# A diffusion backbone's first modulation: three chunks streamed with the vectors stationary, one summed by VectorE, h in two parts, and pair 1's sums between its panels

## Chip, cores, metric

The kernel runs on one core of a Trainium2 chip. The metric is the device time of one execution in microseconds.

## The reference, cut to what matters

Two layers act on 512 latent and 256 context tokens of width 1024, in float32. Each layer has nine modulation vectors per token kind; they come from a vector `c` (latent) or `c_ctx` (context) and a 1024 x 9216 matrix. The first half FFN needs vectors 0 (shift), 1 (scale) and, at its end, 2 (gate) of layer 0.

```
mx = (silu(c) @ ada_w[i] + ada_b[i]).reshape(B, 1, N_MOD, D_MODEL)
mc = (silu(c_ctx) @ ada_w[i] + ada_b[i]).reshape(N_MOD, D_MODEL)
h  = rms_norm(x, norm_g[i, 0]) * (1.0 + mx[:, :, 1]) + mx[:, :, 0]
u  = h @ w_gu
x  = x + 0.5 * mx[:, :, 2] * ((silu(u[..., :D_FF]) * u[..., D_FF:]) @ w_down)
```

After four such half FFNs, one attention and pooling mixer and one recurrent mixer (RG-LRU, whose decay rates come from a softplus of a small vector `lam`) comes a final norm.

## The kernel before

Features lie on the 128 partitions and tokens along the free axis. `resid` holds x and ctx as 8 tiles of 128 x 768. Each engine has its own program; they meet only through semaphores. Panels of weights (1024 x 128) are loaded by the SP queue into one of two raw buffers, ScalarE makes a rounded high part (`high`, L738), GpSimd the low part (`low`, L643), and TensorE multiplies in three passes: high by high, high by low, low by high. The activations h have such parts too, `h_hi` and `h_lo`. A panel of 768 tokens is 8 k-tiles x 3 passes x 2 halves of 384 tokens, so 48 matmuls of 384 columns.

**The prologue.** SP loads x and ctx, then the small vectors, then the first 2048 columns of the modulation matrix (`ada_first`) in four chunks of 2 MB (L479): chunks 0 and 1 are the shift, 2 and 3 the scale, 512 columns each. TensorE transposes x (L1729), VectorE copies it to `resid` (L1292), ScalarE squares (L784), VectorE adds up the squares (L1085). Then TensorE takes chunk 0 with the *weights* stationary and the two vectors `cvec` moving, two columns at a time (L1739, 32 products of 128x128 by 128x2), then the column sums of squares (L1674) and the spreading of 1/rms over the partitions (L1684), which lead through VectorE's `statistics` (L1141), and then chunk 1. VectorE meanwhile multiplies and adds up chunks 2 and 3 (`first_ada`, L1256, through `sum_tiles`, L1026), and TensorE adds these sums over partitions with a vector of ones (L1749). A float32 matmul stands in the trace as two records.

When all 16 tiles are in, VectorE adds the bias (L1267), makes `mod_a` (L1016), and then for each token half (384) and each k: scale (`scale_rows`, L1165), high part on ScalarE (L811), low part on VectorE (L1176). In the second half each of these is two instructions, since latent tokens end at column 512. Behind these rows VectorE computes the decay rates for the recurrent layer (L1304 to L1318), after ScalarE's Exp (L891).

**The first panels.** TensorE begins the first half FFN with `first_panels` (L1594): panel A on half 0, panel B on half 0, panel A on half 1, panel B on half 1, each k-tile waiting for its rows of h. The gate panel goes to `pair_a`, the up panel to `pair_b`; the two are pair 0. Then `gate_up` (L1629) runs pairs 1 to 10. Pair 0 and every later pair end with `use_ada` (L1619): 4 products (8 records) with ones that turn the sums of the next two modulation tiles into columns. VectorE makes such sums in `sum_ada` (L1041) at the head of each pair, and takes the result at the pair's end (`take_ada`, L1046).

**The SP queue's order.** Of each pair SP issues the load of panel A, then `load_ada` (L489), which waits until the previous sums are made, and then the load of panel B. So B's load stands behind VectorE's sums. After the loop of pairs come the down panels `dn00`, then the second half of the FFN, `gu01` and `dn01`.

## Time and profile before

| | us |
|---|---|
| median of 3 runs | 2909.53 |
| range of the runs | 2909.39 to 2911.92 |
| the profiled execution, own time | 2915.29 |
| its span, first to last instruction | 2913.5 |
| TensorE busy in the span | 2767.8 (95%) |
| VectorE busy | 1485.7 (51%) |
| ScalarE busy | 772.6 (27%) |
| GpSimd busy | 896.8 (31%) |
| mean granted TensorE clock, 1 = 2.4 GHz | 0.967 |

PE is TensorE's matmuls, PEld its weight loads, DVE VectorE, ACT ScalarE, POOL GpSimd, SPq the queue on which SP issues DMAs. In a timeline each row is a group of like instructions: its start, the time from its first start to its last end, engine, line, operation, and in brackets how long the engine was idle before it and what ended that. A busy TensorE is not TensorE at its full clock: the granted clock has to be read beside it.

### The profile page before, as it was taken

Reading aid. Unit: us, or ns where it says so; the run is one execution under the profiler, and the core shown is the slowest. Engines: PE = TensorE matmul, PEld = TensorE weight load, DVE = VectorE, ACT = ScalarE, POOL = GpSimd, SP = SyncE. Lnnn points to the kernel's source line nnn. Section 1 sums busy time; section 2 is a strip of 40 time slices with the busy share of each in tenths; the row PEclk is TensorE's granted clock in tenths of the full one; section 3 lists DMA queues with packets and bytes.
Section 4 is the critical chain, followed back from the end, with each engine's and each line's share of the span. In section 5 each row is a group of like instructions: output and inputs, shape, how many; then the busy total and the mean of one; then the engine's idle time right before and its main releaser. Section 6 shows DMA issues by size and latency. Waiting matters only on the chain.

```text
span 2913.5 us, 40217 instructions
## 1 busy us (share of the span) xinstructions
PE 2767.8 (95%) x15161; PEld 2597.9 (89%) x15161; DVE 1485.7 (51%) x2553; ACT 772.6 (27%) x1039; POOL 896.8 (31%) x360
## 2 busy tenths in 40 slices
PE   6799999999999989999999999999998887899998
PEld 6799999998965989999999899999997775778887
DVE  5655555655535366655665523522238887432233
ACT  1322111112145232211111322111125665332222
POOL 0133222332222223322332223222223444244442
PEclk6899999999999999999999999999998997999999
DMA  5244334432210234434443122312211112223332
GB/s 197 58 127 129 111 101 126 127 100 69 68 61 19 65 88 115 123 100 116 115 123 107 44 65 80 107 58 61 75 52 40 55 54 57 70 86 107 88 101 79
DMA packets 413083, 256.77 MB, mean 88 GB/s; under 512 B 6653, under 2 KB 405846, under 8 KB 413014
## 3 DMA queue, kind: packets, MB, share of 16 engines
q1 hardware_dynamic: 413014, 255.87, 30.4%
q8 instruction: 40, 0.66, 0.1%
q14 instruction: 29, 0.24, 0.0%
HBM read 252.70 MB, written 4.25 MB: 88 GB/s over the span
## 4 chain that ended last, share of the span: by engine, by line
PE 65%; issue 19%; DVE 6%; POOL 5%; ACT 4%; DMA 0%; SPq 0%; POOLq 0%; DVEq 0%; ACTq 0%
PE pair_b L1575 28%; PE pair_a L1575 28%; POOL w_lo L647 5%; PE pair_c L1625 2%; PE pair_c L1854 1%; PE pair_a L1815 1%; DVE decay L1535 1%; PE pair_b L1829 1%; DVE decay L1533 1%; PE pair_a L1565 1%; DVE gate_i L1529 1%; DVE h_lo L1176 1%; DVE root L1527 1%; ACT decay L975 1%; ACT root L977 1%
## 5 line engine op out<-in xcount | busy, mean ns | idle before, releaser
L647 POOL TENSOR_TENSOR w_lo<-raw,w_hi 128x1024 fp32r<-128x1024 f32 (+3 forms) x302 | 829.5, 2748 | 1796.7 <-ACT w_hi L750 1796.7
L750 ACT ACTIVATE w_hi<-raw 128x1024 fp32r<-128x1024 f32 (+3 forms) x302 | 337.2, 1117 | 1281.1 <-PE pair_b L1575 443.7
L1067 DVE TENSOR_TENSOR work_g<-work_s,pair_b 128x768 f32<-128x768 f32 (+1 forms) x88 | 78.1, 888 | 702.2 <-PE pair_b L1575 539.7
L1037 DVE SCALAR_TENSOR_TENSOR ada_sums<-ada_raw,cvec,ada_sums 128x256 f32<-128x256 f32 x896 | 395.7, 515 | 0.0
L1575 PE MATMUL pair_a<-h_hi,w_hi 128*128 128x384 f32 x1312 | 338.3, 338 | 9.6 <-POOL w_lo L647 9.6
L1575 PE MATMUL pair_a<-h_lo,w_hi 128*128 128x384 f32 x1312 | 333.6, 335 | 0.0
L1575 PE MATMUL pair_a<-h_hi,w_lo 128*128 128x384 f32 x1312 | 333.6, 335 | 0.0
L1575 PE MATMUL pair_b<-h_hi,w_hi 128*128 128x384 f32 x1168 | 297.7, 335 | 5.9 <-POOL w_lo L647 5.9
L1575 PE MATMUL pair_b<-h_hi,w_lo 128*128 128x384 f32 x1168 | 297.6, 335 | 0.0
L1575 PE MATMUL pair_b<-h_lo,w_hi 128*128 128x384 f32 x1168 | 297.5, 335 | 0.0
L1575 PEld LDWEIGHTS pair_a<-h_hi,w_hi 128*128 128x128 f32 x1312 | 234.5, 189 | 13.5 <-issue 9.6
L1575 PEld LDWEIGHTS pair_a<-h_lo,w_hi 128*128 128x128 f32 x1312 | 237.5, 188 | 0.0
L1575 PEld LDWEIGHTS pair_a<-h_hi,w_lo 128*128 128x128 f32 x1312 | 237.5, 188 | 0.0
L1575 PEld LDWEIGHTS pair_b<-h_hi,w_hi 128*128 128x128 f32 x1168 | 211.7, 189 | 6.5 <-POOL w_lo L647 6.5
L1575 PEld LDWEIGHTS pair_b<-h_lo,w_hi 128*128 128x128 f32 x1168 | 211.9, 189 | 0.0
L1575 PEld LDWEIGHTS pair_b<-h_hi,w_lo 128*128 128x128 f32 x1168 | 211.9, 189 | 0.0
L1098 DVE SCALAR_TENSOR_TENSOR resid<-pair_b,mod_g,resid 128x512 f32<-128x512 f32 (+3 forms) x74 | 42.3, 603 | 314.4 <-PE pair_b L1575 245.2
L1565 PE MATMUL pair_b<-h_hi,w_hi 128*128 128x512 f32 (+3 forms) x352 | 140.0, 398 | 33.3 <-DVE gelu L1514 33.1
L1073 DVE TENSOR_TENSOR g_lo<-work_g,g_hi 128x768 f32 (+1 forms) x88 | 147.3, 1673 | 10.8
L1566 PE MATMUL pair_b<-h_lo,w_hi 128*128 128x512 f32 (+3 forms) x352 | 137.5, 391 | 0.0
L1565 PE MATMUL pair_a<-h_hi,w_hi 128*128 128x512 f32 (+2 forms) x280 | 115.7, 413 | 22.8 <-DVE h_lo L1176 19.2
L1567 PE MATMUL pair_b<-h_hi,w_lo 128*128 128x512 f32 (+3 forms) x352 | 136.8, 389 | 0.0
(272 smaller groups left out, 4548.5 us busy)
## 6 DMA issues: line engine op xcount, KB each, us to landing
raw<-in_ffn_w_gu_dram SPq DMA_DIRECT2D x176, 512.0 KB, 3.9
ada_raw<-in_ada_w_dram SPq DMA_DIRECT2D x64, 1024.0 KB, 5.2
raw<-in_ffn_w_down_dram SPq DMA_DIRECT2D x64, 704.0 KB, 5.5
raw<-in_rg_w_in_dram SPq DMA_DIRECT2D x20, 512.0 KB, 3.8
ada_first<-in_ada_w_dram SPq DMA_DIRECT2D x4, 2048.0 KB, 18.0
raw<-in_ab_w_in_dram SPq DMA_DIRECT2D x16, 512.0 KB, 3.8
raw<-in_rg_w_out_dram SPq DMA_DIRECT2D x8, 640.0 KB, 4.6
raw<-in_ab_w_out_dram SPq DMA_DIRECT2D x8, 512.0 KB, 4.1
```

The costliest lines, as they stand in the source:

```text
L647: nc.gpsimd.tensor_tensor(wl[:, par, 0:kt * P], raw[:, par, 0:kt * P], wh[:, par, 0:kt * P].bitcast(F32), ALU.subtract).then_inc(split_rea ...
L750: nc.scalar.activation(wh[:, par, 0:kt * P], raw[:, par, 0:kt * P], ACT.Copy).then_inc(hi_done, 1)
L975: nc.scalar.activation(decay[d][:, :], gate_r[d][:, :], ACT.Exp, bias=rg_scale[:, m:m + 1], scale=rg_scale[:, m:m + 1])
L1037: step = nc.vector.scalar_tensor_tensor(out=sums[v], in0=tiles(k), scalar=c_k, in1=sums[v], op0=ALU.mult, op1=ALU.add)
L1067: nc.vector.tensor_tensor(gbuf[:, 0, 0:W], sbuf[:, 0, 0:W], up, ALU.mult)\
L1073: nc.vector.tensor_tensor(gl[:, ds(i, 1), 0:W].rearrange("p o n -> p (o n)"), gbuf[:, 0, 0:W], gh[:, ds(i, 1), 0:W].rearrange("p o n -> p ...
L1098: return nc.vector.scalar_tensor_tensor(out=resid[:, k, a:b], in0=src, scalar=mod_g[:, SITE[name], k, v:v + 1], in1=resid[:, k, a:b], op0= ...
L1565: nc.tensor.matmul(dst, w1, hi, start=start, stop=False)
L1566: nc.tensor.matmul(dst, w1, lo, start=False, stop=False)
L1567: return nc.tensor.matmul(dst, w2, hi, start=False, stop=stop)
L1575: last = nc.tensor.matmul(tokens(ps, a, a + HALF), w, of[:, k, a:a + HALF], start=begins, stop=ends)
L1625: last = nc.tensor.matmul(pC[:, 2 * t + v:2 * t + v + 1], ada_sum[:, v, t * P:(t + 1) * P], ones[:, 0:1], start=True, stop=True)
```

## The change

- **TensorE.** Chunks 2, 3 and 1 are now taken with the two vectors stationary (a 128x2 operand) and 512 columns of weights moving, 8 products each, into a 2 x 512 row block of PSUM (`ada_rows`). ScalarE copies each block to SBUF (`copy_ada0`) and TensorE turns it into four 128x2 columns (`turn_ada`).
- **VectorE** sums chunk 0 only, in two parts of four k with `statistics` between.
- **Order.** SP loads chunks 2, 0, 3 ahead of the first two weight panels and chunk 1 behind them. TensorE: chunk 2, both sums of squares, chunk 3, its turning and both spreadings, chunk 0's sums, chunk 1, the last turnings.
- **h in two parts.** k 0 to 3 of both token halves are made once the first four shift and scale tiles are there, k 4 to 7 of both halves after the rest; `row_number` gives the new counts.
- **GpSimd** waits for VectorE's chunk 0 sums before the first low part.
- **Pair 1** is written out: `use_ada(8)`, formerly after pair 0, stands between its panels A and B.
- **Decay rates** with their Exp move from ahead of the first FFN to behind `dn00`.

```diff
@@ -217,7 +217,8 @@
         pro = alias(h_at, g_at)
         xin = pro("x_rows", [P, T // P, D])
         rowbuf = pro("vector_rows", [P, 3, P])
-        ada0_sum = pro("ada_first_sums", [P, 2, 2, ADA0_W])
+        ada0_sum = pro("ada_first_sums", [P, 2, ADA0_W])
+        ada0_row = at("ada_first_rows", [P, 3, ADA0_W], F32, h_at + size([P, KD, T]) + size([P, KD // 2, T]))
         ada0 = alias(g_at, g_end)("ada_first", [P, KD, 2 * ADA0 * P])
...
@@ -305,6 +306,11 @@
         ada_landed = sem("ada_landed")
         ada_summed = sem("ada_summed")
         ada0_summed = sem("ada0_summed")
+        ada0_mm = sem("ada0_mm")
+        ada0_copied = sem("ada0_copied")
+        ada0_turned = sem("ada0_turned")
+        mods_first = sem("mods_first")
+        coef_first = sem("coef_first")
...
@@ -403,6 +409,12 @@
         def norm_tiles_before(i):
             return sum(width(name) // P for name in NORMS[:i])
 
+        def row_number(i, half, k):
+
+            if i > 0:
+                return KD * (2 * i + half) + k
+            return k // 4 * KD + half * 4 + k % 4
+
...
@@ -476,9 +488,14 @@
             rows(lam.rearrange("o d (k p) -> (o d k) p", p=P), R_LAM, 2 * KR)
             assert landed[0] == ROW_DMAS, landed[0]
             w0 = ada_w[0].rearrange("(k p) n -> p k n", p=P)
-            for i in range(4):
+
+            def load_ada0(i):
                 chunk = slice(i * ADA0_W, (i + 1) * ADA0_W)
                 sp.dma_start(ada0[:, :, chunk], w0[:, :, chunk]).then_inc(ada0_landed[i], 16)
+
+            load_ada0(2)
+            load_ada0(0)
+            load_ada0(3)
...
@@ -518,6 +535,7 @@
                     if p0 == 0:
                         load(0, 0, KD, gu[:, :, 0:P])
                         load(1, 1, KD, gu[:, :, DFF:DFF + P])
+                        load_ada0(1)
                         load_ada(ADA0, ADA0, 0)
                         pad_rpb()
                     with_ada(ada_first.get(f"gu{f}{h}"), int(p0 == 0), KC, gate_up)
...
@@ -660,6 +678,7 @@
                 pairs(first[f"gu{f}1"], 0, KC, KD)
                 pairs(first[f"dn{f}1"], 0, KD // 2, KC)
 
+            pool.wait_ge(ada0_summed, 2 * KD)
             ffn(0)
             low(P_AB, 0, KD)
             low(P_AB + 1, 1, KD)
...
@@ -805,7 +824,7 @@
             def high_rows(name, half, k):
 
                 i = NORM_AT[name]
-                act.wait_ge(scaled_done, 2 * KD * i + KD * half + k + 1)
+                act.wait_ge(scaled_done, row_number(i, half, k) + 1)
                 t = shift_tile(i) + k
                 for v, a, b in spans(name, half):
                     last = nc.scalar.activation(hh[:, k, a:b], normed[k % 4][:, a:b], ACT.Identity, bias=mods[:, t, v:v + 1])
...
@@ -868,6 +887,10 @@
                 for h in range(2):
                     gate_up(f, h)
                     outputs(f"dn{f}{h}", first[f"dn{f}{h}"])
+                    if f == 0 and h == 0:
+
+                        act.wait_ge(lam_exp, 1)
+                        nc.scalar.activation(lam_s[:, 1, :], lam_s[:, 0, :], ACT.Exp, scale=-1.0).then_inc(lam_exp, 1)
 
 
             act.wait_ge(cols_done, 1)
@@ -878,17 +901,28 @@
...
@@ -878,17 +901,28 @@
             chain(nc.scalar.activation(sd[:, 7:8], ones[:, 0:1], ACT.Sqrt))
             for k in range(KD):
                 square("in", k)
+
+            def copy_ada0(n, ps, c0):
+
+                act.wait_ge(ada0_mm, n + 1)
+                nc.scalar.activation(ada0_row[0:2, n, :], ps[0:2, c0:c0 + ADA0_W], ACT.Copy).then_inc(ada0_copied, 1)
+
+            copy_ada0(0, pR, 512)
             for half in range(2):
                 root_half("in", half)
             high(0)
             high(1)
+            copy_ada0(1, pB, 0)
+            act.wait_ge(coef_first, 2)
+            for half in range(2):
+                for k in range(4):
+                    high_rows("in", half, k)
+                    if half == 1 and k == 1:
+                        copy_ada0(2, pB, 512)
             act.wait_ge(coef_done, 2)
             for half in range(2):
-                for k in range(KD):
+                for k in range(4, KD):
                     high_rows("in", half, k)
-
-            act.wait_ge(lam_exp, 1)
-            nc.scalar.activation(lam_s[:, 1, :], lam_s[:, 0, :], ACT.Exp, scale=-1.0).then_inc(lam_exp, 1)
             ffn(0)
 
 
...
@@ -1023,9 +1057,9 @@
                 nc.vector.tensor_scalar(mod_g[:, site, :, :], mods[:, t:t + KD, :], 1.0 if site % 3 == 1 else 0.5, None,
                                         ALU.mult).then_inc(coef_done, 1)
 
-            def sum_tiles(tiles, sums, signal, before):
-
-                for k in range(KD):
+            def sum_tiles(tiles, sums, signal, before, ks=range(KD)):
+
+                for k in ks:
                     for v in range(2):
                         n = 2 * k + v
                         c_k = cvec[:, k, v:v + 1]
...
@@ -1160,7 +1194,7 @@
                     dve.wait_ge(rbc_done, norm_tiles_before(i) + half_of(name, half)[1] // P)
                 if k >= 4:
 
-                    dve.wait_ge(h_ready, 2 * KD * i + KD * half + k - 3)
+                    dve.wait_ge(h_ready, row_number(i, half, k - 4) + 1)
                 for v, a, b in spans(name, half):
                     last = nc.vector.scalar_tensor_tensor(out=normed[k % 4][:, a:b], in0=resid[:, k, a:b],
                                                           scalar=mod_a[:, i, k, v:v + 1], in1=halved(pR, name, a, b),
...
@@ -1253,26 +1287,73 @@
                 nc.vector.memset(pT[:, :, PADW - 8:PADW], 0.0).then_inc(proj_done, 1)
                 nc.vector.memset(pT[:, :, PAD_X + SEQ:PAD_C], 0.0).then_inc(proj_done, 1)
 
-            def first_ada():
+            def take_ada0(g):
+
+                tiles = slice(4 * g, 4 * g + 4)
+                src = pC[:, 0:4 * ADA0].rearrange("p (s t v) -> p s t v", s=2, v=2)
+                for v in range(2):
+                    last = nc.vector.tensor_tensor(mods[:, 0:2 * ADA0, v].rearrange("p (s t) -> p s t", s=2)[:, :, tiles],
+                                                   src[:, :, tiles, v],
+                                                   cols[:, 0:2 * ADA0].rearrange("p (s t) -> p s t", s=2)[:, :, tiles], ALU.add)
+                last.then_inc(mods_first if g == 0 else mods_done, 1)
+                dve.wait_ge(mods_first if g == 0 else mods_done, 1)
+                done = coef_first if g == 0 else coef_done
+                for v in range(2):
+                    nc.vector.scalar_tensor_tensor(out=mod_a[:, 0, tiles, v], in0=mods[:, KD:2 * KD, v][:, tiles], scalar=1.0,
+                                                   in1=cols[:, R_NORM:R_NORM + KD][:, tiles], op0=ALU.add, op1=ALU.mult)\
+                        .then_inc(done, 1)
+                dve.wait_ge(done, 2)
+
+            def first_rows():
 
                 dve.wait_ge(silu_done, 1)
+                dve.wait_ge(ada0_landed[0], 16)
+
+                def sums(ks):
+                    sum_tiles(lambda k: ada0[:, k, 0:ADA0_W], [ada0_sum[:, v, :] for v in range(2)], ada0_summed, 0, ks)
+
+                sums(range(4))
+                dve.wait_ge(ss_done, 2)
                 for half in range(2):
-                    dve.wait_ge(ada0_landed[2 + half], 16)
-                    c0 = (2 + half) * ADA0_W
-                    sum_tiles(lambda k: ada0[:, k, c0:c0 + ADA0_W], [ada0_sum[:, half, v, :] for v in range(2)],
-                              ada0_summed, 2 * KD * half)
-                dve.wait_ge(ada_used, 1)
-                src = pC[:, 0:4 * ADA0].rearrange("p (t v) -> p v t", v=2)
-                for v in range(2):
-                    last = nc.vector.tensor_tensor(mods[:, 0:2 * ADA0, v], src[:, v, :], cols[:, 0:2 * ADA0], ALU.add)
-                last.then_inc(mods_done, 1)
-
-                dve.wait_ge(mods_done, 1)
+                    statistics("in", half)
+                sums(range(4, KD))
+                for g in range(2):
+                    if g == 0:
+                        dve.wait_ge(ada0_turned, 1)
+                    else:
+                        dve.wait_ge(ada_used, 1)
+                    take_ada0(g)
+                    for half in range(2):
+                        for k in range(4 * g, 4 * g + 4):
+                            scale_rows("in", half, k)
+                            if k % 4:
+                                low_rows("in", half, k - 1)
+                        low_rows("in", half, 4 * g + 3)
+
+            def decay_rates():
+
+                dve.wait_ge(lam_exp, 2)
...
```

## Rows read from the trace of the kernel before

**Rows 1.** The profile's page: busy time of each engine, share of the span, instructions.
```profile
PE 2767.8 (95%) x15161; PEld 2597.9 (89%) x15161; DVE 1485.7 (51%) x2553; ACT 772.6 (27%) x1039; POOL 896.8 (31%) x360
```
**Rows 2.** Timelines of the prologue, and two 512-column float32 products of a later stage.
```profile
25.95 13.65 PE L1739 MATMUL pair_c<-cvec,ada_first 128*128 128x2 f32 x64
...
70.36 3.57 PE L1749 MATMUL pair_c<-ones,ada_first_sums 128*128 128x1 f32 x16 [6.20 <-DVE ada_first_sums L1037]
...
825.58 1.02 PE L1795 MATMUL pair_c<-p_t,pool_weights 128*128 128x512 f32 x2
826.44 0.59 PE L1796 MATMUL pair_c<-p_t,pool_weights 128*128 128x256 f32 x2
```
**Rows 3.** Windows: length, busy PE, PEld, DVE, ACT, POOL, clock, DMA share, GB/s.
```profile
50.00:60.00 10.00, 10.00 (x49) 10.00 (x48) 10.00 (x14) 0.00 (x0) 1.08 (x1) 0.50 0.18 52
...
82.00:84.00 2.00, 2.00 (x9) 1.47 (x9) 1.85 (x5) 0.61 (x1) 0.00 (x0) 0.77 0.00 0
...
103.00:105.00 2.00, 0.00 (x0) 0.00 (x0) 2.00 (x7) 0.00 (x0) 0.00 (x0) 0.60 0.00 0
...
860.00:880.00 20.00, 20.00 (x108) 12.09 (x108) 10.99 (x38) 10.76 (x27) 1.30 (x3) 1.00 0.03 7
```
**Rows 4.** The tile `ada_first`: time from issue to landing of its four loads.
```profile
DMA to landing us min/median/max: 12.5/18.0/19.9
```
**Rows 5.** Timeline of the prologue: VectorE's steps and the low parts of GpSimd.
```profile
28.05 2.02 DVE L1085 TENSOR_TENSOR sum_sq<-sum_sq,work_s 128x768 f32<-128x768 f32 x2
...
40.92 0.16 DVE L1147 TENSOR_SCALAR mean_sq<-pair_c 128x3 f32<-128x3 f32 x1 [10.86 <-PE pair_c L1674]
...
41.57 0.68 DVE L1153 TENSOR_SCALAR sum_sq<-ident,rstd 128x128 f32<-128x128 f32 x3
...
45.90 2.98 DVE L1033 TENSOR_SCALAR ada_first_sums<-ada_first,cvec 128x512 f32<-128x512 f32 x2
46.09 4.98 POOL L647 TENSOR_TENSOR w_lo<-raw,w_hi 128x1024 fp32r<-128x1024 f32 x2 [44.61 <-ACT w_hi L750]
...
60.16 0.87 DVE L1033 TENSOR_SCALAR ada_first_sums<-ada_first,cvec 128x512 f32<-128x512 f32 x2
```
**Rows 6.** The same timeline from the bias to the decay rates.
```profile
73.97 0.26 DVE L1267 TENSOR_TENSOR mods<-pair_c,cols 128x16 f32<-128x16 f32 x2 [3.66 <-PE pair_c L1749]
...
83.53 1.39 DVE L1165 SCALAR_TENSOR_TENSOR work_s<-resid,mod_a,pair_r 128x128 f32<-128x128 f32 x4
...
95.48 0.18 DVE L1306 TENSOR_SCALAR lam_series<-lam_series 128x20 f32<-128x20 f32 x1 [0.78 <-ACT lam_series L891]
```
**Rows 7.** Timelines from the end of the first panels to pair 2.
```profile
98.78 2.39 POOL L647 TENSOR_TENSOR w_lo<-raw,w_hi 128x1024 fp32r<-128x1024 f32 x1 [47.70 <-ACT w_hi L750]
...
101.66 0.62 DVE L1033 TENSOR_SCALAR ada_sums<-ada_raw,cvec 128x256 f32<-128x256 f32 x2 [0.24 <-DVE rg_tanh L1318]
...
107.87 1.87 PE L1625 MATMUL pair_c<-ones,ada_sums 128*128 128x1 f32 x8 [8.16 <-DVE ada_sums L1037]
107.99 0.38 SPq L494 DMA_DIRECT2D ada_raw<-in_ada_w_dram  x1
...
116.41 1.06 ACT L750 ACTIVATE w_hi<-raw 128x1024 fp32r<-128x1024 f32 x1 [17.70 <-DMA raw<-in_ffn_w_gu_dram]
...
117.54 5.46 POOL L647 TENSOR_TENSOR w_lo<-raw,w_hi 128x1024 fp32r<-128x1024 f32 x1 [16.37 <-ACT w_hi L750]
...
123.06 0.61 PE L1575 MATMUL pair_b<-h_hi,w_hi 128*128 128x384 f32 x2 [3.02 <-POOL w_lo L647]
...
133.87 0.59 PE L1575 MATMUL pair_a<-h_hi,w_hi 128*128 128x384 f32 x2
...
150.59 0.95 PE L1625 MATMUL pair_c<-ones,ada_sums 128*128 128x1 f32 x8
```
**Rows 8.** Timelines of VectorE and TensorE at the boundary from `dn00` to `gu01`.
```profile
387.29 1.14 DVE L1098 SCALAR_TENSOR_TENSOR resid<-pair_b,mod_g,resid 128x512 f32<-128x512 f32 x2 [11.06 <-PE pair_b L1575]
...
412.94 0.51 PE L1575 MATMUL pair_b<-h_hi,w_hi 128*128 128x384 f32 x2
```

More of the change, by code:

```diff
@@ L1745, in _ @@
[L1745 to L1751 removed]
+                for k in range(KD):
+                    last = nc.tensor.matmul(dst, cvec[:, k, :], ada0[:, k, chunk * ADA0_W:(chunk + 1) * ADA0_W],
+                                            start=(k == 0), stop=(k == KD - 1))
```

99 lines of the change are left out of this document (56 added, 43 removed).

## Prediction

> **What bounds the kernel now.** I read the page first: TensorE is busy 95% of the span [rows 1], so only a change to its waits or its slow stretches can move the end. The diff touches the first 134 us and one boundary later, so the second view is the timeline from 0 to 134 us, the third the granted clock in windows, and the fourth who waited for whom. They show that TensorE is busy in the prologue but to little purpose. One chunk of 32 products with the weights stationary takes 13.65 us for 64 records [rows 2], and in such a stretch the engine is busy all of the time at a granted clock of 0.50, the 1.2 GHz level [rows 3]. VectorE needs until 70.3 us for its two chunks (the idle TensorE is released at 70.36 [rows 2]), the bias comes at 73.97, and the rows of h end at 95.48 - 0.78 = 94.70 [rows 6]. The first panels end at 107.87 - 8.16 = 99.71. TensorE then waits 8.16 us for sums, which begin only behind the decay rates at 101.66, and 3.02 us for a low part, whose load SP could issue only behind those sums [rows 7]. Pair 2 starts at 133.87, and from there panels follow each other without a wait. So I work out when pair 2 starts after the change. Whatever it gains there is kept, since TensorE sets the pace behind it.
>
> **The change, step by step.** All times are in the profiled execution's scale.
>
> *Chunk 2, streamed.* The transposes of x are unchanged and end near 26 us, where chunk 0's products begin now (25.95 [rows 2]). The four loads land 12.5 to 19.9 us after their issue [rows 4]; the first is issued at about 6.3 us, so chunk 2 is there by 19 us, chunk 0 by 24 and chunk 3 by 30. A float32 product of 512 columns costs 826.44 - 825.58 = 0.86 us at the full clock, for both records [rows 2]. Eight cost 6.8 us at 2.4 GHz and 13.7 us at 1.2 GHz, which is what the old form costs. The gain hangs on the clock. The nearest rows are on both sides. The old products kept it at 0.50. The attention stage, with float32 products of up to 512 columns, has 1.00 [rows 3]. The first panels restart near 76.7 us and are at the full clock at about 83, inside the window 82 to 84 that shows 0.77 [rows 3]. I take 4.5 us at the low level, then the high one: 2.6 products, then 5.4 x 0.86, so the chunk ends at 35.3.
>
> *Sums of squares and statistics.* VectorE ends its additions at 28.05 + 2.02 = 30.07 [rows 5]. Chunk 0's sums on a free port take from 60.16 to 70.31, 10.15 us [rows 5, 2]; the first half is 4.8 us of it, 30.1 to 34.9, beside TensorE. The twelve records of both sums cost 1.2 us at 0.10 each (0.95 us for eight [rows 7]) and end at 36.5. The two statistics take 42.25 - 40.92 = 1.33 us each [rows 5], to 39.2. Now they wait for a chunk at 0.50; that cover falls away. ScalarE's copy of the first row block, some 0.6 us, falls in between and delays none. Sums 4 to 7 take 5.3 us, to 44.5.
>
> *Chunk 3, turning, spreading, chunk 0's ones.* On TensorE 36.5 + 6.8 = 43.3; four small transposes 0.4, twelve records of spreading 1.3, sixteen of the ones 1.6, all at the full clock: 46.6. No row shows a 2-partition transpose; its bounds are 0.1 and 0.3 us each, of which 0.3 at worst stands on the path four times. Bias and `mod_a` take 0.57 us: 47.2.
>
> *Rows of h.* Bias, `mod_a` and sixteen rows take 94.70 - 73.97 = 20.73 us [rows 6], so 20.2 without the first two. In two groups there are two more ends at which a low part waits for ScalarE; 0.2 to 0.5 us each, I take 0.8 in all, so 10.5 us a group.
>
> *GpSimd's wait.* Now two low parts of 2.49 us each run at 46.09, beside VectorE's sums [rows 5]: that chunk takes 60.16 - 45.90 = 14.26 us instead of 10.15, so 4.1 us go to the collision. After, GpSimd waits until 44.5. Behind that wait stand all its low parts, and the first panel needs the first; it is there at 47 and the panel starts at 54.8, so it costs nothing. But the collision moves on: the low parts run from 44.5 to 49.5, where VectorE starts on h. Bounds 0 and 4.1 us; most of those 5 us VectorE is idle or works with a PSUM operand, so I take 1.8. Group 1 ends at 47.2 + 1.8 + 10.5 = 59.5.
>
> The Trainium skill ("GPSIMD Engine Reference", Specifications) says that GpSimd shares its SBUF interfaces with VectorE, against instructions with two SBUF inputs among others. The longer sums above agree, with 14.26 against 10.15 us. By the rule the scaling rows, with one input in PSUM, would pass and the low rows would be held.
>
> *Chunk 1 and group 2.* TensorE streams chunk 1 from 46.6 to 53.4. ScalarE copies it after the sixth high row, and eight transposes end at 54.8. VectorE is still in group 1, so this has 4.7 us of slack. Take 0.57, rows 10.5: VectorE ends h at 70.6.
>
> *First panels.* Panel A on half 0 runs k 0 to 3 from 54.8, waits for k 4 from 57 to 61.5 and then follows VectorE at 1.05 us a k, to 64.7. That wait may pull the clock down, as the 8.16 us wait does (0.60 in 103 to 105 [rows 3]). Three passes at 1.2 GHz take just under the 1.05 us, so only panel B feels it, by about 0.8 us. Then 3 x 4.15 us: the panels end at 78.1, now 99.71.
>
> *Pair 1.* VectorE sums for it right after h, since the decay rates are gone: 107.81 - 101.66 = 6.15 us [rows 7], 70.8 to 77.0, hidden under the panels. The 8.16 us wait goes. Next in line is the low part of panel 2: it now ends at 101.17 [rows 7], 5.7 us after `pair_a` is full. After, `pair_a` is full at 74.0 and the low part ready at 79.7: a wait of 1.6 us that the sums hid. Panel A takes (150.59 - 133.87) / 2 = 8.36 us [rows 7], to 88.1, and `use_ada` in the middle 0.8, to 88.9. SP can issue the next sums' load and panel 3's at 77.0. The high part begins 116.41 - 107.87 = 8.5 us later [rows 7], at 85.6, ends at 86.7, and the low part takes 2.5 us, not 5.46 [rows 7], as VectorE now waits for `use_ada` till 88.9: ready at 89.2. Panel B runs from 89.2 to 97.5. Its sums start at 89.3 and are made by 95.6, so `use_ada` after it doesn't wait. Pair 2 starts at 98.4 instead of 133.87: 35.5 us earlier. Panel B of pair 2 has its load behind sums that end at 95.6, so its low part is ready at 106.5 or so, when it is wanted; 0 to 1 us, taken as 0. From pair 3 on the loads are ahead as now.
>
> *The boundary.* The decay rates (about 4 us of small steps, 5.9 as they ran [rows 6, 7]) and their wait for Exp now stand behind `dn00`. VectorE is free there at 388.4 [rows 8], the Exp is done near 389.9, the rates by 394 to 396, the sums by 400.2 to 402.2. The load, the high and the low part behind them are ready at 410.7 to 413.1, and TensorE wants them at 412.94 [rows 8]. Its cover is all but used up, and it costs 0 to 0.5 us. I take 0; if the rates took 3 us longer it would cost 3.
>
> **Sum.** 133.9 - 98.4 = 35.5 us. The profiled execution took 2915.29 us, 1.8 us around its span of 2913.5 and 5.8 above the median of the runs. So it would be 2879.8, and against the median 2909.53 - 35.5 = 2874.0.
>
> **The rivals.** *The clock stays low while TensorE streams.* The 2-column operand could leave it at 0.50, as the old products did. Then chunk 2 ends at 39.9, the sums of squares at 42.5, the statistics at 45.1 and the sums of VectorE at 50.4. TensorE has chunk 3 done at 56.1 and the ones at 63.1. Chunk 1 ends at 76.8 and holds up ScalarE's high rows, which stand behind its copy; h ends at 91, 20.5 us later than above. A gain of 15 us, 2894.5.
>
> In the Trainium skill ("TensorE: Matmul & The Clock Gate", Part 1: The HAM clock gate) the clock is set by how busy the engine has been. Taken as busy time alone, the old products would have run at the full clock and the streaming would gain nothing on them. The windows above, busy throughout at 0.50, speak against that reading.
>
> *The gain is eaten behind the weights.* The collision costs 4.1 and the low part of panel 3 takes 5.46 us as now: 2.3 + 3.0 us, with 1 us at pair 2 and 1.5 at the boundary. 28 us gained, 2882.
>
> *Slower than before.* Behind `dn00`, Exp makes ScalarE reload its table in every pair of `gu01`, and VectorE starts late. If each second panel there then came late, the loss would repeat: 11 pairs. It turns the balance from 35.5 / 11 = 3.2 us a pair; at 4 us the time would be 2918. Against it: sums follow the pair's end by 9 us in a pair of 17.5, so a late start heals within a pair.
>
> **How the numbers follow.** Forecast 0.75 (2874, own range 2869 to 2880), eaten 0.10 (2882), low clock 0.11 (2894.5), slower 0.02, and 0.02 for something that takes all back. The low end is no collision (1.8), an earlier clock (1 to 2) and shorter turnings; the upper end of the range takes in the eaten case and a clock that falls again between the chunks, up to 2888. 2868 to 2888 leaves out about 0.2. What this kernel's measurement can tell from no change is about 0.2%, 5.8 us. Faster 0.95, same 0.03, slower 0.02.
>
> **What would show it.** In the trace after: `ada_rows` about 6.8 us a chunk and a clock of 1.00 from 31 us on; h ended near 71; no wait for `ada_sums` in pair 1, one of 1 to 2 us for a low part before its panel A; pair 2 at 98; no wait at the start of `gu01`. I am wrong if the clock reads 0.50 from 30 to 50 us, if VectorE's group 1 lasts 13 us or more, or if TensorE waits again in each pair of `gu01`.

## The result, and the profile after

The kernel after takes 2895.25 us (median of 5 runs, 2891.03 to 2895.87) against 2909.53 before: a ratio of 0.9945, with a 95% interval from 0.9931 to 0.996 (in the experiments the interval stands in square brackets). It is faster by 14.3 us where 35.5 were forecast, and outside the range of 2868 to 2888. A second measurement of the same kernel gave 2897.84. The profiled execution took 2895.85 us (span 2894.1, mean granted clock 0.976), so trace against trace the gain is 19.4 us.

The page's first section of the kernel after:

```profile
PE 2757.6 (95%) x15077; PEld 2569.9 (89%) x15077; DVE 1467.2 (51%) x2541; ACT 786.5 (27%) x1052; POOL 897.0 (31%) x360
```

TensorE is busy 10 us less than in [rows 1], with a share that is still 95%: neither number says where the rest went. The timeline of the prologue, after (start, length, engine, line, operation, idle before and what ended it), first TensorE:

```profile
25.30 7.03 PE L1807 MATMUL pair_r<-ada_first,cvec 128*2 128x512 f32 x16
...
33.69 7.03 PE L1807 MATMUL pair_b<-ada_first,cvec 128*2 128x512 f32 x16
...
42.43 1.93 PE L1831 MATMUL pair_c<-ones,ada_first_sums 128*128 128x1 f32 x16
```

A chunk that took 13.65 us [rows 2] takes 7.03, from the first one on in this trace. Then the steps of VectorE and GpSimd up to pair 1, same timeline:

```profile
36.98 5.38 DVE L1071 SCALAR_TENSOR_TENSOR ada_first_sums<-ada_first,cvec,ada_first_sums 128x512 f32<-128x512 f32 x8
42.44 4.69 POOL L665 TENSOR_TENSOR w_lo<-raw,w_hi 128x1024 fp32r<-128x1024 f32 x2 [40.96 <-DVE ada_first_sums L1071]
44.67 0.23 DVE L1302 SCALAR_TENSOR_TENSOR mod_a<-mods,cols 128x4 f32<-128x4 f32 x2
46.30 1.25 DVE L1210 SCALAR_TENSOR_TENSOR h_lo<-work_s,mods,h_hi 128x384 fp32r<-128x384 f32 x1 [0.22 <-ACT h_hi L830]
56.19 0.23 DVE L1295 TENSOR_TENSOR mods<-pair_c,cols 128x8 f32<-128x8 f32 x2
66.67 0.75 DVE L1210 SCALAR_TENSOR_TENSOR h_lo<-work_g,mods,h_hi 128x128 fp32r<-128x128 f32 x2 [0.22 <-ACT h_hi L830]
67.86 5.63 DVE L1071 SCALAR_TENSOR_TENSOR ada_sums<-ada_raw,cvec,ada_sums 128x256 f32<-128x256 f32 x14
```

h is made by 67.4 us instead of 94.7 [rows 6], and the sums for pair 1 by 73.5 instead of 107.8 [rows 7]. Last, the same timeline from pair 1 to pair 2, all engines:

```profile
77.04 0.62 PE L1634 MATMUL pair_a<-h_hi,w_hi 128*128 128x384 f32 x2 [1.49 <-POOL w_lo L665]
85.47 0.95 PE L1684 MATMUL pair_c<-ones,ada_sums 128*128 128x1 f32 x8
86.69 0.29 DVE L1085 TENSOR_TENSOR mods<-pair_c,cols 128x2 f32 x2 [8.21 <-PE pair_c L1684]
87.78 7.76 DVE L1071 SCALAR_TENSOR_TENSOR ada_sums<-ada_raw,cvec,ada_sums 128x256 f32<-128x256 f32 x14
88.86 2.44 POOL L665 TENSOR_TENSOR w_lo<-raw,w_hi 128x1024 fp32r<-128x1024 f32 x1 [4.38 <-ACT w_hi L769]
96.28 1.74 SPq L504 DMA_DIRECT2D raw<-in_ffn_w_gu_dram  x2
96.52 0.60 PE L1634 MATMUL pair_a<-h_hi,w_hi 128*128 128x384 f32 x2
101.41 5.62 DVE L1071 SCALAR_TENSOR_TENSOR ada_sums<-ada_raw,cvec,ada_sums 128x256 f32<-128x256 f32 x14
102.84 1.06 ACT L769 ACTIVATE w_hi<-raw 128x1024 fp32r<-128x1024 f32 x1 [14.05 <-DMA raw<-in_ffn_w_gu_dram]
103.98 7.58 POOL L665 TENSOR_TENSOR w_lo<-raw,w_hi 128x1024 fp32r<-128x1024 f32 x2 [12.68 <-ACT w_hi L769]
109.29 1.01 PE L1634 MATMUL pair_b<-h_hi,w_hi 128*128 128x384 f32 x2 [4.20 <-POOL w_lo L665]
```

Pair 2 starts at 96.52 instead of 133.87 [rows 7], which is 37.35 us earlier, and 1.9 more than the sum forecast. The gain was there. Read the last line as the first loss: TensorE stands 4.2 us in front of panel B of pair 2 for a low part. Its cause is in the lines above. VectorE gets to the sums of pair 2 only at 87.3 us, since it first takes the result of the `use_ada` in the middle of pair 1 (86.69). Beside the low part of pair 2's panel A (88.86) the 14 running sums take 7.76 us, where alone they take 5.63 (67.86). They are made at 95.5, and panel B's load stands behind them on SP (96.28). The high part comes at 102.84 and the low part at 103.98, just when VectorE makes the next sums (101.41); it takes 5.2 us of the 7.58 that the group of two lasts, where a low part alone takes 2.4. At 2.4 us it would have been ready at 106.4, and TensorE wanted it at 109.29 - 4.20 = 105.09. So of the wait of 4.2 us, by this estimate, 1.3 are the late load and 2.9 the meeting with the sums into which the late load brought it.

To find the others I took the VectorE product that follows each pair's up panel as a milestone, and compared its start in both traces (us):

| stretch | before | after | gain |
|---|---|---|---|
| start to end of pair 0 of `gu00` | 107.72 | 75.59 | 32.1 |
| pair 0 to pair 1 | 25.54 | 19.88 | 5.7 |
| pair 1 to pair 2 | 17.53 | 24.61 | -7.1 |
| pair 0 to pair 1 of `gu01` | 17.53 | 19.91 | -2.4 |
| `gu01` to pair 0 of `gu10` (attention mixer) | 468.93 | 471.47 | -2.5 |
| pair 0 to pair 3 of `gu10` | 59.24 | 64.21 | -5.0 |
| to pair 0 of `gu30` (recurrent mixer) | 448.80 | 451.00 | -2.2 |
| everything else | | | +0.8 |

No other stretch from one milestone to the next differs by more than 0.5 us; what follows the last one is 1.1 us shorter. In `gu10` pair 0 to 1 is 1.7 us shorter and pair 1 to 2 is 6.7 longer. Three of these losses have a wait of TensorE at their head. The same timeline, after, at pair 1 of `gu01` and at pair 2 of `gu10`:

```profile
376.51 5.62 DVE L1071 SCALAR_TENSOR_TENSOR ada_sums<-ada_raw,cvec,ada_sums 128x256 f32<-128x256 f32 x14
378.40 5.93 POOL L665 TENSOR_TENSOR w_lo<-raw,w_hi 128x1024 fp32r<-128x1024 f32 x1 [6.02 <-ACT w_hi L769]
384.39 0.62 PE L1634 MATMUL pair_b<-h_hi,w_hi 128*128 128x384 f32 x2 [2.10 <-POOL w_lo L665]
...
1058.77 0.61 PE L1634 MATMUL pair_b<-h_hi,w_hi 128*128 128x384 f32 x2 [4.28 <-POOL w_lo L665]
```

At `gu01` the low part again began under running sums and took 5.93 us. With 2.4 it would have been ready at 380.8, ahead of the 384.39 - 2.10 = 382.29 at which TensorE wanted it: this wait is the meeting alone. The last line stands in the second half FFN of layer 0, which the change seemed not to touch. It does: the added lines in `gate_up` ask only whether a stage has first panels and makes sums, and `gu10` does both.

```
                    first_panels(p0, after, W, W)
                    start = 1
                    if q0 is not None:
                        tile(1, q0)
                        start = 2
```

So `gu10` too has its `use_ada` between the panels of pair 1, the same late sums in pair 2, and the same wait; there the low part (begun at 1053.36) would alone have been ready at 1055.8, and was wanted at 1054.5.

The losses of the two mixers have no such wait. Windows of 20 us within the attention mixer (length, busy PE, PEld, DVE, ACT, POOL, granted clock, DMA share, GB/s), before:

```profile
820.00:840.00 20.00, 17.14 (x63) 10.33 (x61) 8.14 (x16) 11.80 (x17) 3.34 (x2) 0.93 0.00 1
840.00:860.00 20.00, 20.00 (x91) 12.46 (x90) 8.39 (x31) 8.45 (x21) 4.47 (x5) 0.81 0.03 8
```

and after, at the same place of the program, which comes 28 us earlier:

```profile
792.00:812.00 20.00, 17.58 (x60) 10.41 (x58) 8.23 (x16) 11.80 (x17) 3.10 (x2) 0.87 0.00 0
812.00:832.00 20.00, 20.00 (x77) 12.14 (x76) 7.12 (x25) 7.16 (x18) 2.47 (x3) 0.70 0.03 8
```

The code is the same; the granted clock is down for longer.

### The profile page after: what moved, and what is told of

Read it like the earlier page. It is cut to its first block, busy times and chain, and to the rows that moved or that the text cites. A ratio compares the mean times of both kernels' runs of the same rounds, so it can differ in the third digit from the quotient of the medians.

```text
span 2894.1 us, 40046 instructions
## 1 busy us (share of the span) xinstructions
PE 2757.6 (95%) x15077; PEld 2569.9 (89%) x15077; DVE 1467.2 (51%) x2541; ACT 786.5 (27%) x1052; POOL 897.0 (31%) x360
## 4 chain that ended last, share of the span: by engine, by line
PE 55%; issue 28%; POOL 7%; DVE 6%; ACT 3%; DMA 0%; POOLq 0%; SPq 0%; DVEq 0%; ACTq 0%
PE pair_b L1634 24%; PE pair_a L1634 23%; POOL w_lo L665 7%; PE pair_c L1684 1%; PE pair_c L1940 1%; PE pair_a L1901 1%; DVE decay L1594 1%; PE pair_b L1915 1%; DVE decay L1592 1%; DVE h_lo L1210 1%; DVE gate_i L1588 1%; PE pair_a L1624 1%; DVE root L1586 1%; ACT decay L1009 1%; ACT root L1011 1%
```

## The experiments

Each starts from the kernel after, if nothing else is said, and each computes the whole. Kernels measured side by side share their runs of before. "Pair 1" and "pair 2" in what follows are the milestones of the table. First the theory: *the prologue does what was forecast, and the gain is lost again at three places where a weight load stands behind late sums*. Its rivals: the prologue itself falls short of its worth, or the moved decay rates cost the difference.

**e1, the kernel after again**, in 5 rounds beside e2 to e4, for a base.

> The changed kernel once more, beside the same runs of before, to see how far it and its stages vary. Theory (the gain is given back behind the weights): pair 2 starts at 96.5 us, panel B of pair 2 waits 4.2 us for a low part, pair 1 of gu01 2.1 us, pair 2 of gu10 4.3 us, in every execution; time 2895, 14 us under before. Rival (the missing 21 us are the granted clock, which falls in other places by chance): the waits or the low stretches move or vanish, and the time varies by 5 us or more.

2897.84 us (2895.97 to 2898.36), ratio 0.9953 [0.994, 0.9967]. The two measurements of one kernel differ by 2.6 us, so differences below about 3 us are not read. Pair 1 ended at 98.38 us here and at 95.47 in the first trace: the first streamed chunk began at a low clock and took 8.24 us, and the steps behind it came later; the first panels also stood longer at 0.50 (56 to 64 us, against 60 to 62 in the first trace). From there both run alike. Neither is an exception: in ten traces of kernels with the streamed chunks the first chunk takes 7.03 us in four (after, e2, e5, e7) and 8.1 to 8.6 in six (e1, e3, e4, e9, e10, e11). So "after" below is 2895.3 to 2897.8.

**e2, the `use_ada` in the middle only in `gu00`**

```diff
-                    if q0 is not None:
+                    if q0 is not None and f == 0:
                         tile(1, q0)
                         start = 2
+                    elif q0 is not None:
+                        use_ada(q0)
```

> Pair 1 has its sums between the panels in the first FFN only; gu10, which also has such sums and first panels, uses them after pair 0 as before. Theory: what the row of landmarks shows lost in gu10 (25.9 us ahead before it, 20.9 after it) comes back, 5 us, time 2890. Rival (clock by chance): 2895, no change in the stretch gu10.

2889.24 us (2887.32 to 2893.68), ratio 0.993 [0.9916, 0.9943]. Pairs 0 to 3 of `gu10` take 57.58 instead of 64.21 us, while pair 1 to 2 of `gu00` still takes 25.20. The loss in `gu10` is that line's doing. (The loss at the boundary stays, and varies: pair 0 to 1 of `gu01` takes 21.42 us here.)

**e3, no `use_ada` in the middle anywhere**

```diff
                     if q0 is not None:
-                        tile(1, q0)
-                        start = 2
+                        use_ada(q0)
```

> The sums are used after pair 0 in both FFNs, everything else as changed. Theory: VectorE can begin the next sums about 8 us earlier; panel B of pair 1 then waits about 2 us for a low part that collides with them, but panel B of pair 2 no longer waits 4.2 us and the clock does not fall there; 4 us in the first FFN and 5 in gu10, time 2886. Rival (use between the panels is what hides the sums): TensorE waits for ada_sums after pair 0 and the time is 2895 or more.

2884.24 us (2883.94 to 2886.35), ratio 0.9908 [0.9892, 0.9923]. Pair 1 to 2 takes 17.54 us instead of 24.61. The timeline of TensorE and GpSimd in e3 shows what it trades:

```profile
78.15 0.95 PE L1684 MATMUL pair_c<-ones,ada_sums 128*128 128x1 f32 x8
84.84 5.07 POOL L665 TENSOR_TENSOR w_lo<-raw,w_hi 128x1024 fp32r<-128x1024 f32 x1 [5.09 <-ACT w_hi L769]
89.96 0.62 PE L1634 MATMUL pair_b<-h_hi,w_hi 128*128 128x384 f32 x2 [1.46 <-POOL w_lo L665]
```

With the products back at the end of pair 0 they wait for nothing, since the sums are ready at 76 us (73.5 in after, 76.2 in e3). The next sums start earlier and meet the low part of pair 1's panel B (5.07 us), but that costs a wait of 1.46 us and not 4.2. So by the time that h is early, the place between the panels is no longer needed, and it is what makes the next sums late.

**e4, panel B's load ahead of the load for the sums, on SP**

```diff
                         load(i * 2 + p0, 0, KD, gu[:, :, span(i * P + h * KC * P, P)])
-                        between()
                         load(i * 2 + (p0 + 1), 1, KD, gu[:, :, span(i * P + (DFF + h * KC * P), P)])
+                        between()
```

> The changed kernel with SP's order in each gate and up pair turned round: load A, load B, then the load for the sums, so that no weight panel's load stands behind VectorE's sums. Theory: the waits for low parts in pair 2 (4.2 us and 1.7 us of low clock behind it), in pair 1 of gu01 (2.1 us) and in gu10 (about 5 us) go; time 2881 to 2884. Rival (the low parts are late because GpSimd collides with VectorE, not because the load is late): the waits stay, time 2893 or more. Rival (clock by chance): 2895.

2878.98 us (2878.15 to 2880.48), ratio 0.9892 [0.9877, 0.9907]: 16 to 19 us below after in the medians. The waits of TensorE between 75 and 130 us, after:

```profile
PE pair_b L1634 <- POOL w_lo L665: 4.2, 1, 4.2
PE pair_a L1634 <- POOL w_lo L665: 1.5, 1, 1.5
PE pair_c L1684 <- DVE ada_sums L1071: 0.8, 1, 0.8
```

and in e4 (us in total, times, longest):

```profile
PE pair_a L1634 <- POOL w_lo L665: 1.5, 1, 1.5
PE pair_c L1684 <- DVE ada_sums L1071: 0.8, 1, 0.8
```

The sums are as late as before (their wait of 0.8 us is the same), the load doesn't stand behind them, and the wait for the low part is gone. Pair 1 to 2 takes 17.97 us, `gu01` 17.54, pairs 0 to 3 of `gu10` 57.87. Against e1, beside which it was measured, the three stretches are 15.5 us shorter in sum, of 20.2 us in the spans; the mixers are 5.1 us shorter. All three losses go by one reordering that leaves every computation as it is, so without the late load none of them arises. The rival, that the meeting of GpSimd and VectorE makes the wait and not the load, is refuted as it was put: the waits went with the load. But the two are not separate causes. In e4 the low part of pair 2's panel B runs at 99.10, in 2.39 us and ahead of the next sums, so the reordering took away the lateness and the meeting together; how much of each wait is which is estimated above, and no run splits it. The 5.1 us in the mixers are not shown to be its doing. e3 and e4 remove the wait in `gu00` independently, one by making the sums early, one by taking the load from behind them.

**e5, the decay rates inside `dn00`**, after its second step, where VectorE is idle; the Exp stands ahead of `dn00`'s outputs.

```diff
-                    if f == 0 and h == 0:
-                        decay_rates()
...
+                    if name == "dn00" and k == 1:
+                        decay_rates()
```

> The changed kernel with the decay rates moved from behind dn00 to the second panel of dn00, where VectorE waits some 10 us for TensorE, and with their Exp ahead of dn00. Theory (a late start of VectorE delays a load that stands behind its sums): the 2.1 us wait for a low part in pair 1 of gu01 is gone, from pair 0 to pair 1 of gu01 17.5 us instead of 19.9, time 2.4 us under the changed kernel, 2893 to 2894. Rival (that wait has nothing to do with the decay rates): unchanged.

2891.42 us (2887.22 to 2894.5), ratio 0.9935 [0.9922, 0.9949]. Pair 0 to 1 of `gu01` takes 17.54 us instead of 19.91: the loss at the boundary comes from the decay rates that stand there, ahead of the sums. Here too the low part ran alone, in 2.40 us (at 366.80). e4 cures it as well, because there panel B's load doesn't wait for sums that come late.

**e6, the three chunks with the weights stationary again**, everything else as after.

```diff
-                for k in range(KD):
-                    last = nc.tensor.matmul(dst, cvec[:, k, :], ada0[:, k, chunk * ADA0_W:(chunk + 1) * ADA0_W],
+                for t in range(chunk * ADA0 // 2, (chunk + 1) * ADA0 // 2):
+                    for k in range(KD):
+                        last = nc.tensor.matmul(pC[:, 2 * t:2 * t + 2], ada0[:, k, t * P:(t + 1) * P], cvec[:, k, :],
...
-            copy_ada0(0, pR, 512)
```

> The changed order and split, but chunks 2, 3 and 1 taken as before the change, with the weights stationary and the two vectors moving; no copies of row blocks and no turning, as the result stands in columns at once. Theory (the streamed form is what keeps TensorE at the full clock): the clock falls to 0.50 during chunk 2 and stays there, each chunk takes 13.6 us instead of 7.0, the rows of h start some 13 us later and the time is 2905 to 2915. Rival (the work is the same at either level, and the clock, 1.00 when the chunk begins, stays up): each chunk takes 6.8 us and the time is 2894.

2908.2 us (2901.96 to 2911.43), ratio 0.9993 [0.9984, 1.0002]. So by the medians the streaming is worth 10 to 13 us, and without it the rest of the change shows no gain over before. By the milestones it is worth more: pair 0 ends at 92.22 us, against 75.59 (after) and 78.49 (e1), while the mixers happen to be 6 us shorter than in these. The timeline of TensorE in e6:

```profile
24.87 11.77 PE L1804 MATMUL pair_c<-cvec,ada_first 128*128 128x2 f32 x64
...
39.06 13.79 PE L1804 MATMUL pair_c<-cvec,ada_first 128*128 128x2 f32 x64
...
59.16 13.82 PE L1804 MATMUL pair_c<-cvec,ada_first 128*128 128x2 f32 x64 [0.33 <-DVE mods L1291]
```

and its windows:

```profile
26.00:28.00 2.00, 2.00 (x16) 2.00 (x15) 2.00 (x3) 1.11 (x2) 0.00 (x0) 0.73 1.07 370
30.00:70.00 40.00, 39.67 (x187) 39.58 (x187) 21.77 (x53) 7.75 (x16) 4.66 (x2) 0.50 0.31 101
```

The clock is at its full level when these products begin, after the transposes. It has fallen by 30 us, and stays at 0.50 for 40 us in which the engine is busy 39.67. Under the streamed products at the same place it stays at 1.00: after's windows show 1.00 in each from 20 to 58 us. The form of the product decides it, and one chunk costs 13.8 against 7.03 us. Why it does, no run tells. Where the clock had already fallen, under waits of 0.86 us between the transposes, it rose again under the streamed products: e1 has 0.50 at 26 to 28 us, 0.91 at 28 to 30 and 1.00 from 30 on.

**e7, without GpSimd's wait for chunk 0's sums**

```diff
-            pool.wait_ge(ada0_summed, 2 * KD)
```

> GpSimd does not wait for VectorE's chunk 0 sums; its first two low parts start at about 37 us. Theory (they collide with the sums): the second half of the sums takes 9 to 10 us instead of 5.4, h ends 3 to 4 us later, and pair 2 starts 3 to 4 us later; time 2898. Rival (the two engines share the time without loss, or GpSimd gives way): the sums take 5.4 us and nothing moves.

2899.52 us (2898.63 to 2901.97), ratio 0.9967 [0.9955, 0.9979]: 2 to 4 us above after, and no run of it is as short as the longest of the ten of after (2898.36). In its timeline:

```profile
36.69 9.57 DVE L1070 SCALAR_TENSOR_TENSOR ada_first_sums<-ada_first,cvec,ada_first_sums 128x512 f32<-128x512 f32 x8
36.88 5.51 POOL L665 TENSOR_TENSOR w_lo<-raw,w_hi 128x1024 fp32r<-128x1024 f32 x2 [35.40 <-ACT w_hi L768]
```

Eight sums take 9.57 us beside two low parts, and 5.38 without them. That is 4.2 us, the 4.1 us of the prediction. `mod_a` comes 5.5 us later (50.20 against 44.67), and pair 2 ends 3.7 us later.

**e8, the kernel before with e4's order of loads alone**

```diff
-                        between()
                         load(i * 2 + (p0 + 1), 1, KD, gu[:, :, span(i * P + (DFF + h * KC * P), P)])
+                        between()
```

> The kernel before the change with SP's order turned round as in e4: load A, load B, then the load for the sums. It tells how much of e4's gain is there without the change. Theory: before had waits of 3.0 us in pair 1 of the first FFN with 1.7 us of low clock behind it, and of 2.8 us in pair 1 of gu10; they go, time 2901 to 2903. So the order of loads is worth 7 us before the change and 16 after it, and the change is worth 23 with it. Rival (the order of loads is worth the same in both): 2893.

2907.21 us (2905.77 to 2911.65), ratio 0.9991 [0.9982, 1.0], where 2901 to 2903 was expected: a miss. Pair 1 ends 6.2 us earlier than in the trace of before and `gu10`'s stretch is 3.2 us shorter. But the mixers' stretches are 2.3 and 0.9 us longer, and TensorE's wait for the sums grows to 10.26 us:

```profile
106.79 1.44 PE L1625 MATMUL pair_c<-ones,ada_sums 128*128 128x1 f32 x6 [10.26 <-DVE ada_sums L1037]
```

It also shows something of the base: by its span it is 8.4 us below the trace of before (2905.1 against 2913.5), by the medians 3.1. Most of the difference is that the one profiled execution of before was 5.8 us above its median.

**e9, h in one part**: both takes of the modulation first, then k 0 to 7 of each half, in the old order of rows.

```diff
-            if i > 0:
-                return KD * (2 * i + half) + k
-            return k // 4 * KD + half * 4 + k % 4
+            return KD * (2 * i + half) + k
...
                     take_ada0(g)
-                    for half in range(2):
-                        for k in range(4 * g, 4 * g + 4):
...
+                for half in range(2):
+                    rows_of("in", half, 0, KD)
```

> The changed kernel with h in one part: VectorE takes the second half of the modulation before the first row of h, and makes k 0 to 7 of the first token half, then of the second, as before the change. Theory (VectorE's rows of h are the path, so rows begun before chunk 1 is in are a gain): rows start at 54 us instead of 44.9 and end some 7 us later than the 67 of the changed kernel, TensorE's first panels end some 3.4 us later, and the product of pair 1 comes 4 to 6 us later; time 2900. Rival (chunk 1 hides under the rows in either order): h ends at 67 as now, time 2895.

2901.41 us (2895.23 to 2902.84), ratio 0.9966 [0.9953, 0.9978]: by the medians the two parts are worth 4 to 6 us, though three of the seven runs (2895.2 to 2895.8) are no longer than after. By the milestones it is 4 to 7 us (pair 2 ends at 127.05, against 123.10 in e1 and 120.08 in after), while the mixers of the one profiled execution, at 2895.23, happen to be 5 to 7 us shorter. h ends at about 74.9 instead of 67.4 us, and the sums that follow it then meet pair 1's first low part:

```profile
83.27 1.01 PE L1623 MATMUL pair_a<-h_hi,w_hi 128*128 128x384 f32 x2 [3.31 <-POOL w_lo L663]
```

**e10, the decay rates at their old place**, behind h and ahead of the first FFN.

```diff
             first_rows()
+            decay_rates()
             ffn(0)
...
-                    if f == 0 and h == 0:
-                        decay_rates()
```

> The changed kernel with the decay rates and their Exp back ahead of the first FFN. Theory: VectorE's sums for pair 1 end about 6 us later, the load behind them too, so panel B of pair 1 waits about 5 us for its low part; the 2.4 us in pair 1 of gu01 come back; time 2898, 3 us over the changed kernel. Rival (the sums have 2 us of cover under the panels and use_ada stands between the panels, so the rates cost nothing there): 2893, 2 us under it.

2891.6 us (2887.61 to 2895.49), ratio 0.9939 [0.9925, 0.9953], nearer to the rival. In the timeline, the sums of pair 1 now start behind the rates and run into the low part of its panel A:

```profile
75.51 5.63 DVE L1069 SCALAR_TENSOR_TENSOR ada_sums<-ada_raw,cvec,ada_sums 128x256 f32<-128x256 f32 x14
77.60 5.73 POOL L665 TENSOR_TENSOR w_lo<-raw,w_hi 128x1024 fp32r<-128x1024 f32 x1 [29.52 <-ACT w_hi L769]
83.39 1.01 PE L1631 MATMUL pair_a<-h_hi,w_hi 128*128 128x384 f32 x2 [4.86 <-POOL w_lo L665]
```

Pair 1 ends at 103.36 us against 98.38 in e1, 5.0 us later; 0.6 come back in pair 2, 2.4 at `gu01` and 1.7 in `gu10`. By that sum it should be level with after; the median is 4 to 6 us lower, with mixer stretches that are 5.9 us shorter (468.88 and 448.44 us against 471.53 and 451.72 in e1). So neither theory holds as it was put: the milestones show moving the rates to be worth about nothing, and 5.9 of the 6.6 us by which its span is shorter than that of e1 lie in the mixers, by their clock.

**e11, e3, e4 and e5 together**

> The changed kernel with SP's loads of both panels ahead of the load for the sums (e4), the sums used after pair 0 (e3) and the decay rates in dn00 (e5). Theory (the use between the panels was a cover for a wait that the changed prologue removed, and with the loads first neither form waits long): 1 to 3 us under e4, 2876 to 2878, with pair 1 to pair 2 of the first FFN at 17.5 us and gu10 0 to 3 at 56. Rival (with the loads first the three edits remove the same waits and one of them waits anew): 2879 or more.

2875.66 us (2874.23 to 2876.87), ratio 0.9883 [0.9868, 0.9897]: 20 to 22 us below after and 34 below before. Waits of TensorE for low parts and sums from 60 to 1100 us, after:

```profile
PE pair_b L1634 <- POOL w_lo L665: 10.6, 3, 4.3
PE pair_a L1634 <- POOL w_lo L665: 4.8, 2, 3.3
PE pair_c L1684 <- DVE ada_sums L1071: 2.3, 3, 0.9
```

and in e11:

```profile
PE pair_a L1634 <- POOL w_lo L665: 2.0, 2, 1.2
PE pair_c L1684 <- DVE ada_sums L1071: 1.7, 2, 1.1
```

That this is, within 2 us, the time that the prediction gave to the kernel after is a coincidence: it is another kernel, with three edits more.

## Why the prediction was wrong

It was right in the sign, in the mechanism and in the size of what the prologue gives; it was wrong on what lies behind it. The failed step is the price of the low parts of weights whose load stands behind sums: they were taken at the 2.4 to 2.5 us that they last alone, and met VectorE's sums (5.2 us at pair 2, 5.93 at the boundary), and a third such place, in `gu10`, was not looked at. The prediction's own time for the profiled execution was 2879.8 us, and it took 2895.85.

**Right.** *The bound and the streaming.* The gain hung on the clock, and it stayed at 1.00; the rival of a low clock is refuted by the rows of after, and e6 shows what the old form would have cost. The 4.5 us at the low level were not needed, so the chunk ended at 32.3 and not at 35.3. That was luck of this one trace: in six of the ten the clock was low when the streaming began, at a price of 1.1 to 1.6 us for the chunk.

The Trainium skill ("TensorE: Matmul & The Clock Gate", Part 1: The HAM clock gate) lets the clock follow how busy the engine has been. Busy time alone doesn't decide here: 39.67 busy us of 40 stood at 0.50 in e6.

*Sums, statistics, ones, h.* Statistics ended at 37.0 (forecast 39.2), the sums at 42.3 (44.5), `mod_a` at 44.9 (47.2), all 2.1 to 2.3 us early by the clock. (The chunk was 3.0 us early, but the statistics began only when VectorE had made its first sums, at 34.5, where the forecast had them wait for TensorE until 36.5.) Group 1 ended at 56.2 (59.5). The collision cost VectorE 0.6 us in one row (1.25 against 0.62 us at 46.30), not 1.8: only one low row met the low parts. The rows of group 2 took 10.7 us (10.5), and h ended at 67.4 (70.6).

The rule cited from the Trainium skill ("GPSIMD Engine Reference", Specifications), that GpSimd and VectorE contend where VectorE's instruction has two SBUF inputs, agrees with the rows: of the low rows, with two such inputs, the one beside a low part took 1.25 us and not 0.62, while the scaling rows, with one input in PSUM, took 1.14 us for two (at 44.94) beside a low part as well as (at 56.72) beside none.

*First panels and pair 1.* The clock did feel the wait for k 4, as forecast. The windows of after:

```profile
58.00:60.00 2.00, 0.99 (x4) 0.67 (x5) 1.93 (x4) 1.16 (x3) 0.00 (x0) 0.85 0.00 0
60.00:62.00 2.00, 2.00 (x7) 1.77 (x8) 1.85 (x5) 0.61 (x1) 0.00 (x0) 0.50 0.00 0
62.00:64.00 2.00, 2.00 (x11) 2.00 (x10) 1.78 (x6) 1.50 (x4) 0.00 (x0) 0.79 0.00 0
```

The panels end at 75.6 (78.1). The sums are hidden, and the wait for a low part ahead of panel A is 1.49 us (1.6). Pair 2 starts at 96.5 (98.4), though TensorE waits 0.75 us for the sums ahead of it, where the forecast had no wait.

**Wrong, by three steps and one comparison.**

1. *"Panel B of pair 2 has its load behind sums that end at 95.6 … ready at 106.5 or so, when it is wanted; 0 to 1 us, taken as 0."* The sums ended at 95.5, but as forecast only by two errors that cancel: they began at 87.25 and not at 89.3, and took 2.1 us more than the 6.15 of the row, beside a low part. The high part was there at 103.9. The low part was then costed at its free duration. It met the next sums (101.41 to 107.03) and took 5.2 us, to 109.2. And it was wanted at 105.1, not at 98.4 + 8.4 = 106.8. (The prediction's own intervals, 8.5 + 1.1 + 2.5 us behind 95.6, give 107.7 and not 106.5.) The wait was 4.2 us, and then the clock was down:

```profile
108.00:113.00 5.00, 3.71 (x12) 3.71 (x13) 0.00 (x0) 0.24 (x1) 3.56 (x2) 0.50 0.99 302
```

   Together 7.1 us where 0 to 1 stood. The prediction had named both ends of the collision price, 2.49 and 5.46 us, for panel 3, and left it out for the panel where there was no slack. e3 and e4 show that the wait hangs on the late sums and the load behind them; the share of the meeting is the estimate above.

2. *"From pair 3 on the loads are ahead as now."* True, and so the count stopped at pair 3. The lines added to `gate_up` also run in `gu10`, a stage that the prediction never looked at: 5.0 us. e2 shows it.

3. *The boundary, "0 to 0.5 us, I take 0".* The low part of pair 1's panel B came 2.10 us late and the stretch grew by 2.4 us. The rates were not the error: they took 4.7 us (359.10 to 363.75) where 4 to 6 were forecast, and the sums behind them ended at 370.1, 12.6 us after VectorE was free, inside the forecast 11.8 to 13.8. It was the low part again, costed at 2.5 us: it began under the next sums (376.51) and took 5.93. The warning was in the text, that the cover is all but used up, but for longer rates and not for this. e5 takes the wait away by making the sums early.

4. *"Against the median 2909.53 - 35.5."* A sum of one trace was set against the median of other executions. The trace of before was 5.8 us above its median and that of after 0.6 above: 5.2 us of the gain exist between the traces alone. In which stretch before's profiled execution was long, no run here tells: of this kernel there is only one trace.

With the milestones, 7.1 + 2.4 + 5.0 = 14.5 us are the steps 1 to 3, and 4.7 are the clock in the two mixers. From these go 2.3 for the prologue, which was better than forecast at pair 1, and 0.8 for the rest. That makes 16.1 us, the distance from 2879.8 to 2895.85; with the 5.2 of point 4 it is the 21.3 us between forecast and median.

**The mixers' clock** stays open in part. Shown is that their length goes with the time that the clock is down, with the same code: in the attention mixer's stretch 23.9 us below the full clock where it took 468.9 (before), 30.8 where it took 471.5 (after), 24.0 at 468.3 (e4). (The figure is the sum over windows of the time that TensorE must have stood at 0.50 for the mean granted clock that they show.) All thirteen traces of this stretch lie between 468.2 and 471.5 us, and those of the recurrent one between 447.5 and 451.8. Why an execution falls on one side was not settled: e7, which differs from after only at 37 us, is on the long side in both, and e9 and e10 are on the short side.

**The rivals.** "Eaten behind the weights" had the right mechanism at the right engines, but added 1 us at pair 2 and 1.5 at the boundary where 7.1 and 2.4 were lost. The measured 2895.25 us lies within 1 us of the "clock stays low" rival (2894.5). That is chance: its mechanism is refuted, by 7.03 us a chunk at 1.00. "Slower, in each pair of `gu01`" is refuted: only pair 1 there was late, and the next ones took 17.5 us.

## What to carry over

When a prologue gets shorter, follow each queue until its loads are ahead again, not until the first pair is early: the first panel whose load stands behind late vector work pays the whole. When two engines have been seen to hold each other up, give every later meeting of the two its price, above all where there is no slack. A load that needs nothing from a wait belongs ahead of it in its queue; here that one swap was worth as much as the whole change had brought (15.5 us in the three stretches, 16 to 19 in the medians, against 14). In the kernel before, the same swap brought 3 us in the medians, no more than is read here (e8). Before costing an edit in a shared helper, list every stage that satisfies its condition.

## What the runs showed of the chip

- A float32 product with 2 columns moving and 128x128 weights loses the full clock though TensorE is all but never idle (busy 39.67 of 40 us at 0.50), while the same arithmetic with the 2 columns stationary and 512 moving keeps it: 13.8 against 7.03 us for eight k-tiles of 512 weights' columns, at 0.50 and 1.00.
- When GpSimd and VectorE meet, it isn't always VectorE that pays. Two low parts beside eight running sums took 5.51 us instead of 4.69, and the sums 9.57 instead of 5.38 (e7). Where a low part began under running sums of 256 columns, one of the two bore all of it. A low part that began 2.4 to 3.3 us after such sums had begun took 5.1 to 5.9 us instead of 2.4, and the sums kept their 5.62 (after at 103.98 and 378.40, e3 at 84.84, e10 at 77.60). One that began 1.5 to 1.6 us after such sums had begun took 2.44 to 2.57 us, and the sums 7.76 to 7.78 (after at 88.86 and 1038.10). What decides between them, no run tells.
- Two executions of one kernel differed by 2.9 us in the prologue alone (after and e1). The granted clock differed: it had fallen ahead of the first streamed chunk in e1, and stood at 0.50 for longer in its first panels.
